# Latent attention with both row maxima and exponentials ahead of the divides and the next key behind them, a pause of GpSimd at the start, and the mixer's norm by pairs

## The reference

```python
def _mla_attention(q_nope, q_rope, k_nope, k_rope, v):    # 8 heads, 64+32 wide
    ...
        s = (jnp.einsum('bqhd,bkhd->bhqk', q_nope[:, q0:kend], k_nope[:, :kend])
             + jnp.einsum('bqhr,bkr->bhqk', q_rope[:, q0:kend], k_rope[:, :kend]))
        s = jnp.where(mask, s * scale, -jnp.inf)
        p = jax.nn.softmax(s, axis=-1)
        outs.append(jnp.einsum('bhqk,bkhd->bqhd', p, v[:, :kend]))
...
x = first_block(...)   # a recurrent part beside the attention above, layer norm, a state-space layer, layer norm
# second block
a = rmsnorm(h, g_mix)                  # "the mixer's norm"
proj = a @ w_in                        # short convolution and stick-breaking attention
h = h + concat(conv_out, attn) @ w_out
h = h + square(relu(rmsnorm(h, g_mlp) @ w_up)) @ w_down
h = h + sigmoid(rmsnorm(h, g_ple) @ w_gate) * (p @ w_proj)
return rmsnorm(h, g_final)
```

## Time and profile before

| | us |
|---|---|
| median of 3 runs (2759.21 to 2766.43) | 2763.44 |
| the profiled execution's own time | 2762.98 |
| its span, first to last instruction | 2761.1 |
| TensorE busy in the span | 2687.1 |
| latent attention (207 to 415 us of the span) | 208.0 |
| one head of it (heads 2 to 6) | 24.8 to 24.9 |

### The profile page before, as it was taken

The page is one execution under the profiler, slowest core; times in us unless marked ns, Lnnn a source line. Parts: engine busy times, 40 slices in busy tenths (PEclk is TensorE's granted clock), DMA queues, the critical chain, the costliest instruction groups (busy, mean ns, idle before and its releaser), DMA issues.

```text
span 2761.1 us, 31304 instructions
## 1 busy us (share of the span) xinstructions
PE 2687.1 (97%) x12562; PEld 2153.2 (78%) x12562; DVE 1535.0 (56%) x1724; ACT 914.3 (33%) x1166; POOL 996.2 (36%) x1038
## 2 busy tenths in 40 slices
PE   8999999999999999999999999989999999999998
PEld 7877877787887887887666777767888888888886
DVE  6636663778658658569757566674322222222266
ACT  3537870421212112113347656673211001110032
POOL 4633435431432432432422222225433333333342
PEclk9999999999999999999999999999999999999999
DMA  3110003110110110111230000002111111111212
GB/s 133 53 43 31 24 31 103 65 46 16 46 46 16 46 47 24 46 39 37 71 122 24 31 24 31 31 16 100 53 46 49 52 46 50 50 46 53 89 65 76
DMA packets 39929, 139.31 MB, mean 50 GB/s; under 512 B 4400, under 2 KB 4528, under 8 KB 39792
## 3 DMA queue, kind: packets, MB, share of 16 engines
q1 hardware_dynamic: 31392, 110.11, 12.1%
q10 hardware_dynamic: 8400, 27.26, 2.7%
HBM read 124.77 MB, written 12.58 MB: 50 GB/s over the span
## 4 chain that ended last, share of the span: by engine, by line
PE 82%; DVE 11%; ACT 4%; issue 2%; POOL 1%; ACTq 0%; DVEq 0%; POOLq 0%
PE PS L652 62%; PE PS L889 2%; PE PS L982 2%; PE PS L1023 2%; PE PS L788 1%; PE PS L1208 1%; PE PS L1225 1%; PE PS L802 1%; PE PS L1366 1%; PE PS L1025 1%; PE PS L1247 1%; PE PS L929 1%; DVE ssd_x L2410 1%; DVE ssd_a_upto_lo L2392 1%; PE PS L1011 1%
## 5 line engine op out<-in xcount | busy, mean ns | idle before, releaser
L556 POOL CAST w_hi<-w_stage 128x1024 fp32r<-128x1024 f32 x202 | 218.0, 1079 | 1599.8 <-PE PS L652 1241.6
L559 POOL TENSOR_TENSOR w_lo<-w_stage,w_hi 128x256 fp32r<-128x256 f32 x808 | 728.3, 931 | 16.2
L652 PE MATMUL PS<-XH,w_hi 128*128 128x512 f32 x1216 | 385.0, 398 | 6.8 <-DVE XL L2329 2.8
L652 PE MATMUL PS<-XL,w_hi 128*128 128x512 f32 x1216 | 376.4, 391 | 0.0
L652 PE MATMUL PS<-XH,w_lo 128*128 128x512 f32 x1216 | 375.4, 390 | 0.0
L652 PEld LDWEIGHTS PS<-XH,w_hi 128*128 128x128 f32 x1216 | 222.8, 188 | 60.2 <-issue 9.4
L652 PEld LDWEIGHTS PS<-XL,w_hi 128*128 128x128 f32 x1216 | 228.8, 188 | 49.0
L652 PEld LDWEIGHTS PS<-XH,w_lo 128*128 128x128 f32 x1216 | 228.7, 188 | 48.8
L1988 ACT ACTIVATE ffn_t<-ffn_t 128x1024 f32<-128x1024 f32 x32 | 33.9, 1060 | 530.7 <-DVE ffn_t L2761 530.7
L652 PE MATMUL PS<-raw_hi,w_hi 128*128 128x512 f32 x608 | 188.0, 390 | 0.0
L652 PE MATMUL PS<-raw_hi,w_lo 128*128 128x512 f32 x608 | 187.2, 389 | 0.0
(11 more groups left out here) (421 smaller groups left out, 4914.4 us busy)
## 6 DMA issues: line engine op xcount, KB each, us to landing
w_stage<-w SPq DMA_DIRECT2D x202, 512.0 KB, 3.3
H<-x_t ACTq DMA_DIRECT2D x8, 512.0 KB, 8.2
pj_kept<-ple_proj_tiles ACTq DMA_DIRECT2D x8, 512.0 KB, 2.6
h_kept<-H ACTq DMA_DIRECT2D x8, 512.0 KB, 3.4
H<-h_kept ACTq DMA_DIRECT2D x4, 1024.0 KB, 4.9
out_t<-out_tiles SPq DMA_DIRECT2D x16, 256.0 KB, 2.1
x_again<-x_t ACTq DMA_DIRECT2D x12, 256.0 KB, 3.1
ple_proj_a<-pj_kept ACTq DMA_DIRECT2D x1, 2048.0 KB, 8.1
```

The source lines that it names most:

```text
L556: nc.gpsimd.tensor_copy(w_hi[:, slot, :, :], w_stage[:, slot, :, :]).then_inc(s_w_hi, 1)
L559: nc.gpsimd.tensor_tensor(w_lo[:, slot, k:k + 2, :], w_stage[:, slot, k:k + 2, :], w_hi[:, slot, k:k + 2, :].bitcast(F32), ALU.subtract).t ...
L652: mm = nc.tensor.matmul(outs[:, half, :], wt[:, slot, k, :], a[:, k - first, half * HB:(half + 1) * HB], start=(k == whole[0] and wt is w_ ...
```

## The change

GpSimd: after slab 0 it waits until five `XL` tiles are made before it takes slab 1. Attention on ScalarE: `exponentials(u, 1)` comes ahead of `divide(u, 0)`; `divide(u, 3)` and `chunk_hi(u, 3)` come ahead of `k_hi(u + 1)`. Attention on VectorE: `neg_max(u, 1)` and `chunk_lo(u - 1, 9)` come ahead of `invert(u, 0)` and `add_low(u - 1, 1)`; `chunk_lo(u, 3)` ahead of `k_lo(u + 1)`. The mixer's norm on VectorE does two tiles' `scaled` and then their two `low`, and ScalarE does the two projection copies after its second and fourth `norm_hi`. TensorE's and the sync engine's instructions and their order are as before, and no instruction is added or taken away but the one wait.

```diff
-            for n in range(N_HEADS + 2):
+            next_slab(0)
+            pool.wait_ge(s_xlo, 5)
+            for n in range(1, N_HEADS + 2):
                 next_slab(n)
...
 # ScalarE, attention
                 exponentials(u, 0)
                 if u == 0:
                     gated_hi(1)
-                divide(u, 0)
                 if u:
                     chunk_hi(u - 1, 9)
                 exponentials(u, 1)
+                divide(u, 0)
                 divide(u, 1)
...
                 chunk_hi(u, 2)
                 divide(u, 2)
+                divide(u, 3)
+                chunk_hi(u, 3)
                 if more:
                     k_hi(u + 1)
-                divide(u, 3)
-                chunk_hi(u, 3)
                 exponentials(u, 4)
...
 # ScalarE, the mixer's norm
                 norm_hi(mix, k)
-                if k < 2:
-                    proj_copy(6 + k)
-                    proj_out(6 + k)
+                if k in (1, 3):
+                    proj_copy(6 + k // 2)
+                    proj_out(6 + k // 2)
...
 # VectorE, attention
                 neg_max(u, 0)
-                if u:
-                    add_low(u - 1, 1)
-                invert(u, 0)
                 neg_max(u, 1)
                 if u:
                     chunk_lo(u - 1, 9)
+                invert(u, 0)
+                if u:
+                    add_low(u - 1, 1)
                 invert(u, 1)
...
                 invert(u, 3)
                 neg_max(u, 4)
+                chunk_lo(u, 3)
                 if more:
                     k_lo(u + 1)
-                chunk_lo(u, 3)
                 neg_max(u, 5)
...
 # VectorE, the norm with split parts
-                    if k:
-                        finish(k - 1)
-                finish(KT - 1)
+                if split:
+                    for k in range(0, KT, 2):
+                        scaled(k)
+                        scaled(k + 1)
+                        low(k)
+                        low(k + 1)
+                    return
```

More of the change, by code:

```diff
@@ L2333, in shifted, with scaled @@
                     v.tensor_scalar(H[:, k, :], TN[:, k % 2, :], col("ln2_b", k), None, ALU.add).then_inc(s["h"].sem, 1)
-                finish = low if split else shifted
-                for k in range(KT):
+                def scaled(k):
                     if k >= 2:
@@ L2342, in norm_dve @@
                                              op0=ALU.mult, op1=ALU.mult))
+                if split:
[5 more added lines that the diff above has]
+                    return
+                for k in range(KT):
+                    scaled(k)
                     if k:
-                        finish(k - 1)
-                finish(KT - 1)
+                        shifted(k - 1)
+                shifted(KT - 1)
             cv = Tally(dve, s_cv)
```

## The result

The changed kernel took 2787.89 us (median of 4 runs, 2787.05 to 2791.73), the kernel before, run beside it, 2761.32 (4 runs, 2758.92 to 2766.43): a ratio of 1.0098, 95% interval 1.0085 to 1.011. The sign was forecast, the size was not: +26.6 us where 2774 stood for +11.2, and 2787.9 is outside the range.

A forecast was written before the change was run, and what follows sets the result against it. TensorE, busy 2687.1 of 2761.1 us, was taken as the bound. Late key +8.5, head 7 -1.2, norm 0, GpSimd's rest 0 and clock +3.9 gave +11.2 on 2762.98, forecast 2774 us, range 2765 to 2780.

The forecast's parts named there:

- The sign: Whole kernel: the change makes it slower, by +11.2 us; chance of measurably slower 0.62.
- the range: Whole kernel's time: 2765 to 2780 us.
- the price of one fall of the clock: Attention heads: one fall from 2.4 to 1.2 GHz costs 1.3 us, taken from head 1 against head 3.
- The count of falls: Attention heads: the new gap brings 0 to 6 more falls of the clock; three taken.
- the clock's term: Attention heads: three more falls of the clock, +3.9 us, between 0 and +7.8.
- The late key: Seven heads: `k_lo` ends later, so scores 5 start 1.21 us later in each, +8.5 us in all.
- Head 7: Last head: earlier chunk and divides shorten TensorE's wait, -1.2 us, between -0.9 and -1.7.
- Maxima in heads 1 to 6: Attention: earlier maxima and exponentials are worth 0, hidden by the 3 us of the next queries.
- the norm: Mixer's norm: TensorE's wait moves from tile 1 to tile 2, 0 us, between -0.3 and +1.3.
- GpSimd's rest: Start of the kernel: GpSimd waiting before slab 1 is worth 0 us, between -0.4 and +0.3.
- Rival 3: Attention: the clock falls in every head, six more falls, +7.8 us; +15.4 in all, 2778 us; chance 0.12.

The follow-up runs named there:

- experiment 5: Changed kernel with the 24 matmuls of each head's next values widened from 64 to 128 columns, added half unread: 2791.19 us, ratio 1.0114 to the kernel before.
- experiment 2: All of the change but the key's two moves (`k_hi`, `k_lo` put back), against the kernel before: 2760.73 us, ratio 0.9995.
- experiment 9: Changed kernel with values 3 and turn 5 ahead of scores 5 on TensorE: 2773.54 us, ratio 1.0043 to the kernel before.
- experiment 1: Only the key's two moves (`k_hi` and `k_lo` later), on the kernel before: 2779.5 us, ratio 1.0069.
- experiment 7: Changed kernel with six unread matmuls per head in TensorE's gap ahead of scores 5: 2769.88 us, ratio 1.0031 to the kernel before.
- experiment 8: Kernel before with `k_hi` behind `divide(3)` but ahead of `chunk_hi(3)`, VectorE as before: 2770.01 us, ratio 1.0028.
- experiment 3: Kernel before with only both row maxima and exponentials put ahead of the divides: 2760.26 us, ratio 0.9998.
- experiment 4: Kernel before with only GpSimd's rest at the start and the mixer's norm by pairs of tiles: 2761.41 us, ratio 0.9995.
- experiment 11: All of the change, but the key's copy and low part ahead of divide 2 and the fifth maximum, scores 5 ahead of turn 4: 2757.55 us, ratio 0.9981.

## Why the prediction was wrong, step by step

- **The step that failed: the price of one fall of the clock.** "One fall from 2.4 to 1.2 GHz costs 1.3 us there", and three more of them, +3.9. In the kernel after, heads 0 to 6 have four falls where they had one, three more, but these cost 19.2 - 1.3 = +17.9. That gaps in front of TensorE bring falls was right; the price of one, taken from head 1 alone, was not: here it is 4.5 to 5.6 us. In head 1 before, the stretch at the low level was 3.4 us long, in the heads after it is 10.2 us (13.65 in head 2), and half speed for 10.2 us is worth 5.1 us at most. The single row showed one size of a thing that has several, and it was used as both estimate and bound. A second size stood in the trace of before, outside the attention, and was not looked for: TensorE's windows at the low level, two of before,

```profile
257.30:260.71 3.41, 3.41 (x18) 0.50 0.00 0
1861.57:1868.40 6.83, 6.40 (x15) 0.50 0.17 47
```

  and those of heads 4 and 5 after:

```profile
339.44:349.68 10.24, 10.24 (x51) 0.50 0.00 0
370.16:380.40 10.24, 10.24 (x51) 0.50 0.00 1
```

- **The count of falls** (three more): right by luck. Three was the middle of 0 to 6, and no row gave it; experiment 5, with the same gaps, has five in heads 0 to 6. The comparison behind it was also misread: by the prediction's own distances the new gap is 304.93 - 303.1 = 1.83 us (measured, 1.87), so it did not lie between 1.93 and 2.37 but below both. And the length of a gap alone doesn't decide: the gap of 2.0 us in the norm by pairs was followed by a fall of 3.4 us in two traces (experiments 2 and 9) of the eight that have it.
- **The range.** Its upper end was six falls of 1.3 us. With 4.6 in its place the same count gives 28 us and some 2798. Between forecast and result lie 14 us; the clock's term is 14.0 us too small, and the other terms together are off by 1.0.
- **The late key** (+8.5): right. The chain, per head, start of each in the kernel after at the full clock: `divide(2)` and `divide(3)` back to back, then

```profile
309.88 0.47 ACT L1518 ACTIVATE mla_p_hi<-PS 128x384 fp32r<-128x384 f32 x1
310.25 1.00 ACT L1495 ACTIVATE mla_k_hi<-PS 64x1024 fp32r<-64x1024 f32 x1
```

```profile
311.28 1.22 DVE L2163 TENSOR_TENSOR mla_k_lo<-PS,mla_k_hi 64x1024 fp32r<-64x1024 f32 x1 [0.34 <-ACT mla_k_hi L1495]
```

  0.37 from chunk to key, 1.03 to `k_lo`, 1.27 to the scores at 312.55: each as worked out from the earlier trace rows. Head 0 costs 0.8 and not 1.2, for +8.1 in seven. Experiments 1, 7 and 8 confirm the sum: heads of 26.03, 26.01 to 26.03, and 25.65.
- **Head 7** (-1.2): it came to -1.8. Turn 9 to turn 0 takes 4.23 us and took 5.07, close to the -0.86 of the prediction. The rest, about 0.95, fits the clock, which stayed up: the prediction counted half of 0.8 us for it, from a window that ends at 396, but the stretch at the low level went on to 397.25, 3.4 us that are worth 1.7 at most.
- **Maxima in heads 1 to 6, the norm, GpSimd's rest** (0 each): right, by experiments 2 to 4, as far as the median tells (the norm's fall in two of eight traces is the +1.3 that was named as its bound). Slab 1 starts at 23.07 us and started at 22.67; the first lo part was 0.6 us later in this execution, and by the next queries of head 0 the two stand 0.12 us apart (215.22 and 215.10).
- **Rival 3**, a fall in every head, wasn't the case either: three of heads 0 to 6 are at the full clock. It priced a fall at the same 1.3 us, and so its 2778 was too low as well. The Trainium skill ("TensorE: Matmul & The Clock Gate", section "A second HAM failure mode: psum-queue depth-cycling") has a kernel whose TensorE idles briefly and often, and swings between the two levels. The trace agrees as to the swings, and filling the gap (experiment 7) took them away; but the gap comes only once in 26 us here, in heads in which TensorE is 92% busy. I had weighed this rule only as to how often the clock falls, and not as to what a fall costs.

What stays open: why the same gap of 1.87 us is followed by a fall in four heads of seven and not in the others; why some stretches at the low level last 3.4 us and others 10.2 or more; and how far the short gaps of experiment 9 matter. In experiment 1 the two short stretches (3.4 us) began 0.2 us after and 0.1 us before the start of the scores behind the gap, and the two long ones (10.2 us) 0.9 and 1.1 after it; in the kernel after, all four long ones began 0.5 to 1.1 us after it, and in experiment 5 all five 0.8 to 1.6 after it (read from the granted clock in windows of 0.05 us). That is an order seen in 13 cases, without a cause. Narrow matmuls behind the gap aren't it (experiment 5).

## What to carry to other kernels

At 97% TensorE, price a new wait twice: once by the chain that makes it late, which rows of the trace give to a few hundredths of a microsecond, and once by what it may do to the clock, for which one fall seen in the old trace is no bound; here each one cost 3.5 to 4.3 times that. What several engines empty in turn for one that must not stand (here a PSUM pair of the ring) goes ahead of work that has slack, and the waits that this moves are to be put behind work that doesn't need them; experiment 11 is the one case of it here. Where an order must leave a gap, unread matmuls in it are a cheap test of how much of its cost is the clock.

## What was not expected of the hardware

- A TensorE that had been idle for 1.87 us in 26 was, in four heads of seven, at 1.2 GHz for 10.2 to 13.65 us of unbroken work afterwards, and the gap cost 4.5 to 5.6 us beside its own length. With six matmuls in that gap the clock stayed at 1.00 in six heads running.
- A fall need not start in the gap: in the kernel after it came 0.5 to 1.1 us after TensorE had resumed, at the full clock in between, and in experiment 9 it came 3.0 to 3.9 us after.
- Adding work made the kernel faster: 2769.9 us with 42 more matmuls of 512 columns, against 2787.9 without them.
